# Stick-breaking attention starts without a barrier: the first pair's split parts are made in another buffer

## The chip, the cores and the metric

The kernel runs on one core of one Trainium2 chip. Its time is the device time of one launch in microseconds; the time before is the median of three runs.

## The reference, cut to what matters

The whole program is four transformer layers on 512 tokens of width 1024. The change touches the first layer's mixer, one half of which is stick-breaking attention with 8 heads of 64:

```
xr, gr, q, k, v = split(h @ ev_w_in, 5)            # five panels of 512 columns
q, k = rms_norm(q) * gain, rms_norm(k) * gain      # by head
z   = q @ k.T / 8                                  # for each head
sp  = where(kpos < qpos, softplus(z), 0)
rev = reverse cumulative sum of sp over the keys
w   = exp(where(kpos < qpos, z - rev, -inf))
yb  = w @ v
x  += g1 * (concat([ya, yb]) @ ev_w_out)           # ya: the recurrent half
```

## The kernel before

Every engine walks the same list of steps: gemm stages, norms, attention blocks, and barriers ("bar") at which TensorE (PE), ScalarE (ACT) and VectorE (DVE) wait for one another. Each engine runs its own program in order, and semaphores tie them together. `past(n)` is a semaphore's target of n plus a constant.

**Split operands.** All products are made in float32 from two rounded parts, high = round(x) and low = x - high, as three matmuls. For weights ACT makes the high part (L1604), and GpSimd (POOL) the low part by one subtraction of 128x1024 (L849).

**The panels before the attention.** The normalised q, the normalised k and the values are three "panel" stages, each of four units; a unit is 24 matmuls of 128x512 over four token tiles (L999, L1002, L1005). The k tiles are scaled by DVE (L2380), turned by PE (L972) and taken by ACT (L1642) while PE works on the values' panel. Semaphore `h_take` counts the tiles taken. DVE also finishes the recurrent half during the values' panel: scans (L2434), and the low parts of four output chunks (L2441, `lru_low`). ACT copies the four finished value tiles out of PSUM (L1655, semaphores `evac`).

**The attention, `stick`.** Heads come in four pairs. For a pair, q of both heads is one 128x512 tile, and each head's k is 64 rows of a 128x512 tile whose other 64 rows are zero. All these parts lie in `qk_parts`, which is double buffered by pair and shares its memory with `h_hi` and `h_lo`, the operand of the panels. Before the attention stands a barrier, and behind it three engines work at once: POOL zeroes the other rows (`zero_rows`, two memsets of 64x2048, L875), ACT copies the high parts of pair 0 (`high_parts(0)`, L1821 and L1823) and DVE subtracts for the low parts (`low_parts(0)`, L2450 and L2453). PE then makes the scores of head 0 in four chunks, kt = 2, 1, 0, 3 (L1256 to L1259). ACT takes abs, exp and log of each chunk (L1834, L1837, L1840), DVE adds the softplus (L2466), PE adds the suffix sums (L1270, L1271), ACT makes the weights (L1847), PE multiplies by the values (L1279). Each head's scores are begun before the head in front is done. The output of pair i goes to chunks i + 4 of `y_hi` and `y_lo`, which are empty until then.

**The queue of SyncE (SP).** The output projection is the next gemm stage (its `after_stick` is set). SP issues the loads of its first two weight units, waits for the barrier's three semaphores, and then issues 32 loads of the modulation weights (512 KB each, L544) into a ring of four slots in `tmp`; from the fifth on, each waits for a DVE addition (`ada_add`, L555 and L557), of which DVE makes four for each head.

**POOL's program** is in order too: last panel's weight splits, zeroing, then the low part of the projection's first weight unit (L849).

Of the kernel before, what the change touches and what calls it, by code (L numbers as in the profile page):

```python
# [15 lines left out]
P = 128  # L16
S = 512
# [103 lines left out]
def program(nc, a, out):  # L121
# [13 lines left out]
    with ctx:  # L135
# [98 lines left out]
        def parts(mode):  # L234
# [2 lines left out]
                    [[qkt(4 + 4 * par + k) for k in range(2)] for par in range(2)],  # L237
                    [[qkt(6 + 4 * par + k) for k in range(2)] for par in range(2)])

        def dil_q_high(g, p):  # L240


            if g and p % NB == 0:
                return (yhi, ylo)[g - 1][:, 4 * S:6 * S]
            return whi[1][:, :] if g == 0 else qk[:, (4 * (p % 2) + 2 * (g - 1)) * S:(4 * (p % 2) + 2 * g) * S]
# [159 lines left out]
        panel(ev, 2 * LW, 24, S, a["ev_qn_g"], Q_SCALE)  # L405
        panel(ev, 3 * LW, 28, S, a["ev_kn_g"])
        panel(ev, 4 * LW, 32)
        steps += [("bar", None), ("stick", None), ("mods", 0), ("bar", None)]
        STICK_BAR = sum(kind == "bar" for kind, _ in steps) - 1
        gemm_stage("down", 8, DC, a["ev_w_out"][0], "y", gate=16)  # L410
        steps[-1][1].after_stick = True
        steps[-1][1].products, steps[-1][1].ada = (0, [3]), (0, 8, 8)
# [236 lines left out]
        def stick_z(par, kt):  # L649

            return bank[NB * par + kt][:, 0:S - kt * P]

        def stick_out(par):

            return bank[NB * par + NB - 1][64 * par:64 * par + 64, :]
# [84 lines left out]
        @block.sync  # L740
        def _(sp):
            sp.dma_start(extra[0:DC, 0:P], a["c"].rearrange("b (r n) -> (b r) n", n=P)).then_inc(s_c, 16)
            sp.dma_start(sq9[:, :], a["square"]).then_inc(s_const, 16)

            def first_weights(i):
                if i >= 8:
                    sp.wait_ge(s_first, i - 7)
                sp.dma_start(ring_first[i % 8], ada_source(*first_order[i])).then_inc(s_first_w[i % 8], 16)

            for i in range(4):  # L750
                first_weights(i)
            sp.dma_start(zt(6, 8).rearrange("p (b d) -> p b d", b=NB),
                         a["x"][0].rearrange("(b p) d -> p b d", p=P)).then_inc(s_x, 16)
            for i in range(4, FIRST * DC):
                first_weights(i)
            sp.dma_start(raw[0][:, :].rearrange("p (c n) -> p c n", n=P), stages[0].weights[0](0)).then_inc(w_raw[0], 16)
            sp.dma_start(Z[:, 0:N_MASK * P], a["masks"]).then_inc(s_masks, 16)
            sp.wait_ge(s_zgate, 1)

            for w, name in enumerate(("ev_wa", "ev_wx")):  # L760
                for b in range(2):
                    tiles = Z[64 * b:64 * b + 64, 32 * S:34 * S].rearrange("p (t w n) -> p t w n", w=2, n=P)
                    sp.dma_start(tiles[:, :, w, 64 * b:64 * b + 64],
                                 a[name][0].rearrange("(t b) k j -> b k t j", b=2)[b]).then_inc(s_gates, 16)

            def load(st, i, j):
                u = st.base + j + 2 * i
                half = st.base // 2 + i

                sp.wait_ge(s_wlo, past(u - 1))  # L770
                sp.dma_start(raw[j][:, 0:st.kc * P].rearrange("p (c n) -> p c n", n=S if st.kind == "panel" else P), st.weights[j](i)).then_inc(w_raw[j], 16)

            for st in stages:
                lo = 0
                if st.normed:
                    k = st.gain_index
                    if k >= 2:
                        sp.wait_ge(h_tab, past(k - 1))
                    sp.dma_start(gain_rows[:, DH * (k % 2):DH * (k % 2 + 1)], st.gain.to_broadcast([P, DH])).then_inc(s_gain[k % 2], 16)
                if st.base == 0 or st.after_stick:  # L780
                    if st.base:
                        load(st, 0, 0)
                    load(st, 0, 1)
                    lo = 1
                if st.after_stick:

                    for bar in (bar_pe, bar_act, bar_dve):
                        sp.wait_ge(bar, STICK_BAR)
                    for i in range(4 * DC):
                        ada_load(sp, 0, i)  # L790
                if st.ada[1]:
                    for l in range(st.n):
                        if l >= 2 * lo:
                            load(st, l // 2, l % 2)
                        for i in ada_of(st, l):
                            ada_load(sp, 1, i)
                    continue
                if st.n // 2 - lo <= 1 or st.kind == "panel":
                    for i in range(lo, st.n // 2):
                        load(st, i, 0)  # L800
                        load(st, i, 1)
                else:
                    with sp.Fori(lo, st.n // 2) as i:
                        load(st, i, 0)
                        load(st, i, 1)
            for t in range(NB):
                for hh in range(2):

                    sp.wait_ge(s_xc, DC + 2 * t + hh + 1)
                    sp.dma_start(out[0, t * P:(t + 1) * P, hh * S:(hh + 1) * S], zt(2 * t + hh)).then_inc(s_out, 16)  # L810
            sp.wait_ge(s_out, 16 * 2 * NB)
# [3 lines left out]
        def _(pool):  # L815
# [35 lines left out]
            def zero_rows(n_bars, kind):  # L851
# [5 lines left out]
                    todo = [qk[HALF[1 - par], (4 + 4 * par) * S:(8 + 4 * par) * S].rearrange("p (t n) -> p t n", n=2 * S)[:, :, 0:S] for par in range(2)]  # L857
                elif kind == "diff":
                    todo = [qk[64:128, 5 * S:6 * S], qk[64:128, 7 * S:8 * S], qk[0:64, 9 * S:10 * S], qk[0:64, 11 * S:12 * S]]
                else:  # L860
                    todo = [qk[64:128, 4 * S:8 * S], qk[0:64, 8 * S:12 * S]]
                zero(todo)

            def dil(base):
# [15 lines left out]
            for at_step, (kind, st) in enumerate(steps):  # L880
                if kind == "bar":
                    n_bars += 1
                if kind in ("stick", "diff", "window"):
                    zero_rows(n_bars, kind)
                if kind == "dil":
                    dil(st)
                if kind == "diff":
# [47 lines left out]
        def _(pe):  # L935
# [301 lines left out]

            def stick():
                e = stk
                q_hi, q_lo, k_hi, k_lo = parts("stick")  # L1240
                zero_rows_in(2)

                def scores(i, par, chunks):
                    h = 2 * i + par
                    if par == 0:
                        pe.wait_ge(e["low_parts"], past(2 * i + 2))
                    pe.wait_ge(e["weights"], past(4 * (h - 1)))
                    for kt in chunks:
                        if kt == NB - 1:
                            pe.wait_ge(e["output_low"], past(h - 1))  # L1250
                        if kt == 2 and par and i:
                            products(0, [i - 1])
                        z = stick_z(par, kt)
                        kh, kl = (t[par][i % 2][:, kt * P:(kt + 1) * P] for t in (k_hi, k_lo))
                        qh, ql = (t[i % 2][:, kt * P:S] for t in (q_hi, q_lo))
                        pe.matmul(z, kh, qh, start=True, stop=False)  # L1256
                        pe.matmul(z, kh, ql, start=False, stop=False)
                        pe.matmul(z[:, 0:P], identb[:, :], mask(T_S), start=False, stop=False, skip_group_check=True)
# [264 lines left out]
        def _(act):  # L1523
# [289 lines left out]
            def stick():  # L1813
                e = stk

                q_hi, _, k_hi, _ = parts("stick")

                def high_parts(i):

                    act.wait_ge(e["scores"], past(8 * (i - 1)))  # L1820
                    act.activation(q_hi[i % 2], zt(i + 24), ACT.Copy).then_inc(e["high_parts"], 1)  # L1821
                    for r, t in zip(HALF, k_hi):
                        ins = act.activation(t[i % 2][r, :], zrows(r, i + 28), ACT.Copy)  # L1823
                    ins.then_inc(e["high_parts"], 1)

                def logarithm(i, par, chunks):
# [24 lines left out]
                    act.wait_ge(e["values_added"], past(2 * i + par + 1))  # L1851
                    act.activation(ch(yhi, i + 4)[r, :], stick_out(par), ACT.Copy).then_inc(e["output_high"], 1)

                high_parts(0)
                logarithm(0, 0, STICK_ORDER)
                for h in range(8):
                    i, par = divmod(h, 2)
# [269 lines left out]
        def _(dve):  # L2127
# [254 lines left out]
            def panel(st):  # L2382
# [9 lines left out]
                        head_tile(st, b)  # L2392
                if st.index <= 1:
                    lru_scan(range(2 * st.index, 2 * st.index + 2))
                if st.index in (1, 2):
                    lru_low(range(2 * st.index - 2, 2 * st.index))

# [40 lines left out]
            def lru_low(chunks):  # L2438
                for t in chunks:
                    dve.wait_ge(l_y, t + 1)  # L2440
                    dve.tensor_tensor(ch(ylo, t), zt(16 + t), ch(yhi, t), ALU.subtract)  # L2441

            def stick():
                e = stk

                q_hi, q_lo, k_hi, k_lo = parts("stick")

                def low_parts(i):
                    dve.wait_ge(e["high_parts"], past(2 * i + 1))
                    dve.tensor_tensor(q_lo[i % 2], zt(i + 24), q_hi[i % 2], ALU.subtract).then_inc(e["low_parts"], 1)  # L2450
                    dve.wait_ge(e["high_parts"], past(2 * i + 2))
                    for r, high, low in zip(HALF, k_hi, k_lo):
                        ins = dve.tensor_tensor(low[i % 2][r, :], zrows(r, i + 28), high[i % 2][r, :], ALU.subtract)  # L2453
                    ins.then_inc(e["low_parts"], 1)

                def values(i):
                    dve.wait_ge(e["values_added"], past(2 * i))
# [12 lines left out]
                    dve.wait_ge(e["output_high"], past(2 * i + par + 1))  # L2470
                    dve.tensor_tensor(ch(ylo, i + 4)[r, :], stick_out(par), ch(yhi, i + 4)[r, :], ALU.subtract).then_inc(e["output_low"], 1)

                low_parts(0)
                values(0)
                softplus(0, 0, STICK_ORDER)
                for h in range(8):
# [4 lines left out]
                    if par == 0 and i:  # L2481
                        values(i)
                    if par == 0 and i < 3:
                        low_parts(i + 1)
                    for k in range(4 * par, 4 * par + 3):
                        ada_add(dve, 0, i, k)
                    if h < 7:
# [372 lines left out]
```

## Time and profile before

| what | us |
|---|---|
| median of 3 runs | 2951.89 (2949.53 to 2953.6) |
| time of the profiled execution | 2955.01 |
| its span, first to last instruction | 2953.2 |
| values' panel: last matmul starts | 169.95 |
| attention: first score starts | 174.99 |
| attention: last product of weights and values ends | 260.69 |

All positions are microseconds from the start of the span. The profiled execution is 3.1 us above the median of the runs.

### The profile page before, as it was taken

How to read it: one execution, taken by the hardware profiler on the slowest of the kernel's cores; microseconds unless marked ns; L12 is line 12 of the kernel's file. 1: busy time of each engine (PE TensorE's matmuls, PEld its weight loads, DVE VectorE, ACT ScalarE, POOL GpSimd, SP SyncE). 2: the span in 40 equal slices, each digit the busy share in tenths (PEclk: the TensorE clock that was granted, in tenths of full speed). 3: DMA queues.
4: the chain of work that ended last, by engine and by line, in shares of the span. 5: the costliest groups of instructions: out<-in, count | busy, mean ns of one | idle time of the engine just before them, and what ended most of it. 6: DMA issues, size and time to landing. Idle time of an engine off the chain costs nothing.

```text
span 2953.2 us, 39009 instructions
## 1 busy us (share of the span) xinstructions
PE 2845.3 (96%) x13396; PEld 2322.4 (79%) x13396; DVE 1738.4 (59%) x2097; ACT 1224.3 (41%) x2062; POOL 1076.1 (36%) x486
## 2 busy tenths in 40 slices
PE   6989999999899999999879999999999999999999
PEld 4767788887677888888658888888898889888887
DVE  7476777866566554667465334457666766654333
ACT  3564432223554322244453222256556665532221
POOL 1311344443213444444214444444322442244443
PEclk9999999999999999999899999999999999999999
DMA  6245263643112333333003333332311331133332
GB/s 216 87 157 193 79 197 106 203 126 105 41 29 78 98 94 97 90 94 92 29 8 86 99 93 96 97 95 87 93 30 45 94 89 34 44 97 95 95 97 93
DMA packets 366013, 278.96 MB, mean 94 GB/s; under 512 B 13491, under 2 KB 321076, under 8 KB 365876
## 3 DMA queue, kind: packets, MB, share of 16 engines
q1 hardware_dynamic: 364624, 276.83, 31.2%
q8 instruction: 82, 1.34, 0.2%
q14 instruction: 56, 0.45, 0.1%
q10 hardware_dynamic: 1251, 0.33, 0.0%
HBM read 275.03 MB, written 2.10 MB: 94 GB/s over the span
## 4 chain that ended last, share of the span: by engine, by line
PE 67%; DVE 2%; ACT 2%; issue 1%; POOL 0%; DVEq 0%; ACTq 0%; POOLq 0%
PE banks L1131 13%; PE banks L1126 13%; PE banks L1135 12%; PE banks L999 6%; PE banks L1005 6%; PE banks L1002 6%; PE banks L1395 2%; PE banks L972 1%; PE banks L1456 1%; PE banks L1335 1%; PE banks L1128 1%; PE banks L1324 0%; PE banks L1040 0%; PE banks L1370 0%; PE banks L1369 0%
## 5 line engine op out<-in xcount | busy, mean ns | idle before, releaser
L849 POOL TENSOR_TENSOR w_lo<-w_raw,w_hi 128x1024 fp32r<-128x1024 f32 (+1 forms) x423 | 1027.5, 2429 | 1712.3 <-ACT w_hi L1604 1711.3
L1604 ACT ACTIVATE w_hi<-w_raw 128x1024 fp32r<-128x1024 f32 (+1 forms) x424 | 445.6, 1051 | 1124.9 <-PE banks L1135 804.9
L999 PE MATMUL banks<-w_hi,h_hi 128*128 128x512 f32 x960 | 386.4, 403 | 1.4 <-ACT h_hi L1782 1.4
L1005 PE MATMUL banks<-w_lo,h_hi 128*128 128x512 f32 x960 | 376.9, 393 | 0.7 <-POOL w_lo L849 0.7
L1002 PE MATMUL banks<-w_hi,h_lo 128*128 128x512 f32 x960 | 375.9, 392 | 0.7 <-DVE h_lo L587 0.7
L1126 PE MATMUL banks<-h_hi,w_hi 128*128 128x512 f32 x1280 | 340.1, 394 | 6.9 <-ACT h_hi L1782 6.9
L1131 PE MATMUL banks<-h_lo,w_hi 128*128 128x512 f32 x1280 | 321.3, 391 | 2.6 <-DVE h_lo L587 2.4
L1126 PEld LDWEIGHTS banks<-h_hi,w_hi 128*128 128x128 f32 x1280 | 241.7, 189 | 65.2 <-issue 8.7
L1131 PEld LDWEIGHTS banks<-h_lo,w_hi 128*128 128x128 f32 x1280 | 240.3, 188 | 57.9 <-DVE h_lo L587 8.6
L1135 PE MATMUL banks<-h_hi,w_lo 128*128 128x512 f32 x1152 | 284.5, 389 | 0.0
L1135 PEld LDWEIGHTS banks<-h_hi,w_lo 128*128 128x128 f32 x1152 | 216.2, 188 | 44.9
L1126 PE MATMUL banks<-mid_hi,w_hi 128*128 128x512 f32 x864 | 220.3, 394 | 7.2 <-ACT mid_hi L1734 4.7
L1005 PEld LDWEIGHTS banks<-w_lo,h_hi 128*128 128x128 f32 x960 | 196.2, 204 | 35.5 <-POOL w_lo L849 1.5
L999 PEld LDWEIGHTS banks<-w_hi,h_hi 128*128 128x128 f32 x960 | 196.5, 205 | 32.6 <-issue 2.1
L1002 PEld LDWEIGHTS banks<-w_hi,h_lo 128*128 128x128 f32 x960 | 196.9, 205 | 31.8 <-DVE h_lo L587 1.0
L1131 PE MATMUL banks<-mid_lo,w_hi 128*128 128x512 f32 x864 | 218.3, 391 | 2.3 <-DVE mid_lo L2275 2.1
L2292 DVE TENSOR_TENSOR xT<-banks,xT 128x512 f32 (+1 forms) x80 | 55.3, 692 | 273.2 <-PE banks L1135 273.1
L1135 PE MATMUL banks<-mid_hi,w_lo 128*128 128x512 f32 x864 | 214.4, 389 | 0.0
L1126 PEld LDWEIGHTS banks<-mid_hi,w_hi 128*128 128x128 f32 x864 | 160.6, 188 | 45.3 <-ACT mid_hi L1734 8.1
L1131 PEld LDWEIGHTS banks<-mid_lo,w_hi 128*128 128x128 f32 x864 | 162.2, 188 | 41.4 <-DVE mid_lo L2275 4.7
L1135 PEld LDWEIGHTS banks<-mid_hi,w_lo 128*128 128x128 f32 x864 | 162.2, 188 | 33.5
L2380 DVE TENSOR_TENSOR tmp<-tmp,head_sums 128x512 f32<-128x512 f32 (+1 forms) x84 | 133.5, 1589 | 34.2 <-issue 23.2
(343 smaller groups left out, 4256.2 us busy)
## 6 DMA issues: line engine op xcount, KB each, us to landing
Z<-in_ada_w SPq DMA_DIRECT2D x64, 512.0 KB, 5.0
w_raw<-in_m_w_up SPq DMA_DIRECT2D x64, 512.0 KB, 4.0
w_raw<-in_m_w_down SPq DMA_DIRECT2D x64, 512.0 KB, 3.8
w_raw<-in_kv_w SPq DMA_DIRECT2D x48, 512.0 KB, 3.7
w_raw<-in_ffn_w_gate SPq DMA_DIRECT2D x44, 512.0 KB, 3.7
w_raw<-in_ffn_w_up SPq DMA_DIRECT2D x44, 512.0 KB, 3.7
tmp<-in_ada_w SPq DMA_DIRECT2D x32, 512.0 KB, 4.5
w_raw<-in_ffn_w_down SPq DMA_DIRECT2D x32, 512.0 KB, 3.8
```

The lines of the kernel that those rows point to most:

```text
L849: pool.tensor_tensor(wlo[j][:, 0:n], raw[j][:, 0:n], whi[j][:, 0:n], ALU.subtract).then_inc(s_wlo, 1)
L972: mm = pe.transpose(turned(n)[:, j * P:(j + 1) * P], tmp[4 + n % 2][:, j * P:(j + 1) * P], ident)
L999: pe.matmul(t, hh, wh, start=k == 0, stop=False)
L1002: pe.matmul(t, hl, wh, start=False, stop=False)
L1005: mm = pe.matmul(t, hh, wl, start=False, stop=k == DC - 1)
L1126: pe.matmul(g, whi[par][:, k * P:(k + 1) * P], hi[:, k * S:(k + 1) * S], start=(k == 0), stop=False)
L1131: mm = pe.matmul(g, whi[par][:, k * P:(k + 1) * P], lo[:, k * S:(k + 1) * S], start=False, stop=early and k == st.kc - 1)
L1135: mm = pe.matmul(g, wlo[par][:, k * P:(k + 1) * P], hi[:, k * S:(k + 1) * S], start=False, stop=(k == st.kc - 1))
L1395: mm = pe.matmul(o, dil_vals[:, at:at + P], dil_probs[q % 2][:, own:own + width], start=g == 0 and c == 0, stop=g == 2 and c == NB - 1, sk ...
L1604: act.activation(whi[par][:, 0:kc * P], raw[par][:, 0:kc * P], ACT.Copy).then_inc(s_whi, 1)
L2292: dve.tensor_tensor(x, G[par], x, ALU.add).then_inc(evac[par], 1)
L2380: dve.tensor_tensor(by_head(tmp[4 + n % 2], w), roped, scale, ALU.mult).then_inc(h_out, 1)
```

## The change

The first barrier goes. Pair 0's parts are made in chunks 5, 6 and 7 of `y_hi` and `y_lo`, all of them on DVE within its part of the values' panel. POOL zeroes the rows of `qk_parts` once the panel's last matmul is done; PE waits for that only at head 2, the first head that reads `qk_parts`. PE waits for the copies of the value tiles before its second chunk. SP issues the modulation weights' loads once all q and k tiles are taken.

```diff
+        def first_parts():
+            return ch(yhi, 5), ch(ylo, 5), [ch(yhi, 6), ch(yhi, 7)], [ch(ylo, 6), ch(ylo, 7)]
...
-        steps += [("bar", None), ("stick", None), ("mods", 0), ("bar", None)]
-        STICK_BAR = sum(kind == "bar" for kind, _ in steps) - 1
+        steps += [("stick", None), ("mods", 0), ("bar", None)]
+        stick_values = panels[-1]
...
+        def stick_parts(i):
+            if i == 0:
+                return first_parts()
+            q_hi, q_lo, k_hi, k_lo = parts("stick")
+            return q_hi[i % 2], q_lo[i % 2], [t[i % 2] for t in k_hi], [t[i % 2] for t in k_lo]
...
                 if st.after_stick:
-                    for bar in (bar_pe, bar_act, bar_dve):
-                        sp.wait_ge(bar, STICK_BAR)
+                    sp.wait_ge(h_take, past(stick_values.tiles))
...
-                if kind in ("stick", "diff", "window"):
+                if kind in ("diff", "window"):
                     zero_rows(n_bars, kind)
+                if kind == "stick":
+                    pool.wait_ge(gemm, past(stick_values.base + stick_values.n))
+                    zero([qk[64:128, 4 * S:8 * S], qk[0:64, 8 * S:12 * S]])
...
             def stick():                                   # PE
-                zero_rows_in(2)
+                pe.wait_ge(h_take, past(stick_values.tiles))
                 def scores(i, par, chunks):
                     h = 2 * i + par
+                    q_hi, q_lo, k_hi, k_lo = stick_parts(i)
+                    if h == 2 and chunks[0] == STICK_ORDER[0]:
+                        zero_rows_in(2)
...
+                        if h == 0 and kt == 1:
+                            for b in range(NB):
+                                pe.wait_ge(evac[b % 2], past(tile_evac(stick_values, b) + 1))
...
-                high_parts(0)                              # ACT
                 logarithm(0, 0, STICK_ORDER)
...
                 if st.index <= 1:                          # DVE, panel
                     lru_scan(range(2 * st.index, 2 * st.index + 2))
+                if st is stick_values:
+                    stick_first()
                 if st.index in (1, 2):
                     lru_low(range(2 * st.index - 2, 2 * st.index))
...
             def lru_low(chunks):
                 for t in chunks:
                     dve.wait_ge(l_y, t + 1)
-                    dve.tensor_tensor(ch(ylo, t), zt(16 + t), ch(yhi, t), ALU.subtract)
+                    ins = dve.tensor_tensor(ch(ylo, t), zt(16 + t), ch(yhi, t), ALU.subtract)
+                link(ins)
+
+            def stick_low(i):
+                e = stk
+                q_hi, q_lo, k_hi, k_lo = stick_parts(i)
+                dve.wait_ge(e["high_parts"], past(2 * i + 1))
+                dve.tensor_tensor(q_lo, zt(i + 24), q_hi, ALU.subtract).then_inc(e["low_parts"], 1)
+                dve.wait_ge(e["high_parts"], past(2 * i + 2))
+                for r, high, low in zip(HALF, k_hi, k_lo):
+                    ins = dve.tensor_tensor(low[r, :], zrows(r, i + 28), high[r, :], ALU.subtract)
+                ins.then_inc(e["low_parts"], 1)
+
+            def stick_first():
+                q_hi, _, k_hi, k_lo = stick_parts(0)
+                for c in range(2):
+                    for t in (k_hi[c], k_lo[c]):
+                        dve.memset(t[HALF[1 - c], :].bitcast(F32), 0.0)
+                dve.wait_ge(h_take, past(stick_values.tiles))
+                dve.wait_ge(h_out, past(stick_values.tiles))
+                dve.tensor_copy(q_hi, zt(24)).then_inc(stk["high_parts"], 1)
+                for r, t in zip(HALF, k_hi):
+                    ins = dve.tensor_copy(t[r, :], zrows(r, 28))
+                ins.then_inc(stk["high_parts"], 1)
+                stick_low(0)
...
-                low_parts(0)                               # DVE, stick
+                for b in range(NB):
+                    dve.wait_ge(evac[b % 2], past(tile_evac(stick_values, b) + 1))
                 values(0)
                 softplus(0, 0, STICK_ORDER)
```

`link` makes DVE wait until its own instruction has written.

## Rows read from the trace of the kernel before

**Rows 1.** The page, busy time of PE: us, share of the span, instructions.
```profile
PE 2845.3 (96%) x13396; PEld 2322.4 (79%) x13396; DVE 1738.4 (59%) x2097; ACT 1224.3 (41%) x2062; POOL 1076.1 (36%) x486
```

**Rows 2.** Timeline, PE, 152 to 186: start, us, what, [idle before, releaser].
```profile
169.95 0.39 PE L1005 MATMUL banks<-w_lo,h_hi 128*128 128x512 f32 x1
174.99 0.55 PE L1256 MATMUL banks<-qk_parts 128*128 128x256 f32 x1 [4.64 <-POOL qk_parts L875]
...
178.87 0.34 PE L1256 MATMUL banks<-qk_parts 128*128 128x256 f32 x1
...
182.09 0.49 PE L1271 MATMUL banks<-Z,squares 128*128 128x128 f32 x2 [1.04 <-DVE Z L2466]
```

**Rows 3.** Timeline, POOL and SP, 152 to 186.
```profile
171.12 3.66 POOL L875 MEMSET qk_parts<- 64x2048 f32 x2 [9.00 <-ACTq L1548]
175.01 2.36 POOL L849 TENSOR_TENSOR w_lo<-w_raw,w_hi 128x1024 fp32r<-128x1024 f32 x1 [0.23 <-POOL qk_parts L875]
...
171.08 14.87 SPq L544 DMA_DIRECT2D tmp<-in_ada_w  x5
```

**Rows 4.** Timeline, ACT, 152 to 186.
```profile
165.47 0.58 ACT L1642 ACTIVATE Z<-banks 128x512 f32<-128x512 f32 x1
...
170.38 0.60 ACT L1655 ACTIVATE Z<-banks 128x512 f32<-128x512 f32 x1 [0.40 <-PE banks L1005]
171.17 0.63 ACT L1821 ACTIVATE qk_parts<-Z 128x512 fp32r<-128x512 f32 x1 [0.20 <-issue]
171.71 1.25 ACT L1823 ACTIVATE qk_parts<-Z 64x512 fp32r<-64x512 f32 x2
176.24 0.39 ACT L1834 ACTIVATE Z<-banks 128x256 f32<-128x256 f32 x1 [3.29 <-PE banks L1259]
```

**Rows 5.** Timeline, DVE, 152 to 186.
```profile
167.77 2.49 DVE L2441 TENSOR_TENSOR y_lo<-Z,y_hi 128x512 fp32r<-128x512 f32 x4
171.93 0.69 DVE L2450 TENSOR_TENSOR qk_parts<-Z,qk_parts 128x512 fp32r<-128x512 f32 x1 [1.68 <-ACT qk_parts L1821]
172.99 1.39 DVE L2453 TENSOR_TENSOR qk_parts<-Z,qk_parts 64x512 fp32r<-64x512 f32 x2 [0.36 <-ACT qk_parts L1823]
174.41 0.65 DVE L2458 TENSOR_SCALAR Z<-Z 128x512 f32<-128x512 f32 x1
177.56 0.42 DVE L2466 SCALAR_TENSOR_TENSOR Z<-banks,Z 128x256 f32<-128x256 f32 x1 [2.50 <-ACT Z L1840]
```

**Rows 6.** Timeline, DVE and POOL, 2117 to 2128, a later stage with the same forms.
```profile
2118.14 0.42 DVE L2645 CAST y_hi<-Z 64x512 fp32r<-64x512 f32 x1
2118.61 0.48 DVE L2644 MEMSET y_lo<- 64x512 f32 x1
2119.11 1.99 DVE L2645 CAST y_lo<-Z 64x512 fp32r<-64x512 f32 x1
...
2118.36 2.46 POOL L849 TENSOR_TENSOR w_lo<-w_raw,w_hi 128x1024 fp32r<-128x1024 f32 x1 [4.00 <-ACT w_hi L1604]
```

**Rows 7.** The same stretch, where POOL comes up between two DVE subtractions.
```profile
2123.13 0.68 DVE L2563 TENSOR_TENSOR Z_rounded<-Z,y_hi 128x512 fp32r<-128x512 f32 x1
2123.73 2.89 DVE L2563 TENSOR_TENSOR Z_rounded<-Z,y_lo 128x512 fp32r<-128x512 f32 x1
...
2123.51 2.55 POOL L849 TENSOR_TENSOR w_lo<-w_raw,w_hi 128x1024 fp32r<-128x1024 f32 x1 [2.69 <-ACT w_hi L1604]
```

**Rows 8.** Timeline, DVE and POOL, 2167 to 2169.
```profile
2167.60 0.82 DVE L2690 CAST w_hi<-Z 64x512 fp32r<-64x512 f32 x1 [2.69 <-PE banks L1005]
...
2167.63 0.52 POOL L875 MEMSET w_hi<- 64x512 f32 x1 [11.14 <-PE banks L1005]
2168.21 0.69 POOL L875 MEMSET w_lo<- 64x512 f32 x1
```

**Rows 9.** Windows just after PE restarts: stretch, us, busy by engine, PEclk (granted share), DMA.
```profile
174.90:178.20 3.30, 3.21 (x12) 2.32 (x12) 0.58 (x2) 1.86 (x5) 2.36 (x1) 0.50 0.94 364
...
1434.30:1441.10 6.80, 6.80 (x28) 5.48 (x28) 3.48 (x6) 1.83 (x8) 0.20 (x1) 0.50 0.00 0
```

More of the change, by code:

```diff
@@ L859, in zero_rows @@
                     todo = [qk[64:128, 5 * S:6 * S], qk[64:128, 7 * S:8 * S], qk[0:64, 9 * S:10 * S], qk[0:64, 11 * S:12 * S]]
-                else:
-                    todo = [qk[64:128, 4 * S:8 * S], qk[0:64, 8 * S:12 * S]]
                 zero(todo)
@@ L1239, in stick @@
                 e = stk
-                q_hi, q_lo, k_hi, k_lo = parts("stick")
-                zero_rows_in(2)
+                pe.wait_ge(h_take, past(stick_values.tiles))
                 def scores(i, par, chunks):
                     h = 2 * i + par
+                    q_hi, q_lo, k_hi, k_lo = stick_parts(i)
+                    if h == 2 and chunks[0] == STICK_ORDER[0]:
+                        zero_rows_in(2)
                     if par == 0:
@@ L1252, in scores @@
                             products(0, [i - 1])
+                        if h == 0 and kt == 1:
+                            for b in range(NB):
+                                pe.wait_ge(evac[b % 2], past(tile_evac(stick_values, b) + 1))
                         z = stick_z(par, kt)
-                        kh, kl = (t[par][i % 2][:, kt * P:(kt + 1) * P] for t in (k_hi, k_lo))
-                        qh, ql = (t[i % 2][:, kt * P:S] for t in (q_hi, q_lo))
+                        kh, kl = (t[par][:, kt * P:(kt + 1) * P] for t in (k_hi, k_lo))
+                        qh, ql = (t[:, kt * P:S] for t in (q_hi, q_lo))
                         pe.matmul(z, kh, qh, start=True, stop=False)
@@ L1814, in stick @@
                 e = stk
-                q_hi, _, k_hi, _ = parts("stick")
                 def high_parts(i):
+                    q_hi, _, k_hi, _ = stick_parts(i)
                     act.wait_ge(e["scores"], past(8 * (i - 1)))
-                    act.activation(q_hi[i % 2], zt(i + 24), ACT.Copy).then_inc(e["high_parts"], 1)
+                    act.activation(q_hi, zt(i + 24), ACT.Copy).then_inc(e["high_parts"], 1)
                     for r, t in zip(HALF, k_hi):
-                        ins = act.activation(t[i % 2][r, :], zrows(r, i + 28), ACT.Copy)
+                        ins = act.activation(t[r, :], zrows(r, i + 28), ACT.Copy)
                     ins.then_inc(e["high_parts"], 1)
@@ L2440, in lru_low @@
                     dve.wait_ge(l_y, t + 1)
-                    dve.tensor_tensor(ch(ylo, t), zt(16 + t), ch(yhi, t), ALU.subtract)
+                    ins = dve.tensor_tensor(ch(ylo, t), zt(16 + t), ch(yhi, t), ALU.subtract)
[21 more added lines that the diff above has]
+                stick_low(0)
             def stick():
                 e = stk
[L2446 to L2454, printed above, removed]
                 def values(i):
@@ L2483, in stick @@
                     if par == 0 and i < 3:
-                        low_parts(i + 1)
+                        stick_low(i + 1)
                     for k in range(4 * par, 4 * par + 3):
```

## The prediction

> **What bounds the kernel now.** I read the page's busy times first: PE is busy for 96% of the span [rows 1], so a change pays where it takes time out of PE's row and not elsewhere. Then the timeline of PE around the barrier that goes. The values' panel ends at 169.95 + 0.39 = 170.34, the first score starts at 174.99, and the row gives 4.64 us of idle time, released by POOL's memset [rows 2]. That hole is all that the change can remove. Its neighbours show what fills it. ACT copies the last value tile at 170.38, then makes the high parts until 171.71 + 1.25 = 172.96 [rows 4]. DVE makes the low parts until 172.99 + 1.39 = 174.38 [rows 5]. POOL zeroes from 171.12 to 171.12 + 3.66 = 174.78 [rows 3]. Three waits end there, POOL's last, DVE's only 0.4 us ahead of it. The first thing to see: taking POOL off this path alone is worth 0.4 us, because DVE is next in line.
>
> Behind the first score (call its start T) comes a chain that a later start shifts as a whole: first softplus on DVE at T + 2.57 (177.56) [rows 5], first suffix sum at T + 7.10 (182.09), where PE has waited 1.04 us for DVE [rows 2].
>
> **Part by part: when can DVE deliver?** The high parts move from ACT to DVE, so T now hangs on DVE alone. ACT is rid of 0.63 + 1.25 us of copies [rows 4], which is worth nothing by itself: it then sat idle 3.29 us before its first abs [rows 4].
>
> *What stands in front on DVE.* The k tiles are all taken at 165.47 + 0.58 = 166.05 [rows 4], well within the panel. But DVE is busy with the recurrent half: its four L2441 subtractions begin at 167.77, one each 0.61 (from 2.49 for four, the last taking 0.69) [rows 5]. Two of them stay in front of the new work and end at 167.77 + 0.61 + 0.69 = 169.07; the other two move behind it. The new `link` adds a wait of DVE for its own write. I estimate it at 0.2 us, as POOL's end to PE's start (174.78 to 174.99) [rows 2, 3], bounds 0 and 0.3. So the new work starts at 169.3.
>
> *Four memsets of 64x512.* One takes 0.48 and its follower starts 0.50 later [rows 6]; with an overlap as L2441 has, 0.41. I take 0.45: 1.8 us, until 171.1. The last two meet POOL. The row at 2118.61 is such a memset beside POOL's subtraction and took its 0.48 [rows 6]; beside a POOL memset no row shows one. I take no delay; were the third held as a copy is, all behind it would queue once more, 1.3 us for bound (its own end at 172.5, and three copies behind L849).
>
> *Three copies.* A CAST of 64x512 takes 0.42 [rows 6], and the 128x512 one has as many elements in a partition, so undisturbed they are 3 x 0.42 = 1.3 us. They are not undisturbed. POOL no longer waits for a barrier but for the panel's last matmul, 170.34, and starts at about 170.42, as ACT's value copy, released by the same matmul, did at 170.38 [rows 4] (bounds 170.4 and 170.6). Its two memsets are 1.8 us each [rows 3], so POOL writes from 170.4 to 174.1 at least, just where DVE copies. The trace shows what a copy does then. The cast at 2119.11 comes while POOL's subtraction (2118.36 to 2120.82) runs, takes 1.99 in place of 0.42 and ends 0.28 after POOL [rows 6]. The cast at 2167.60 stands beside a POOL memset, ends at 2168.42, 0.27 after that memset's end at 2168.15; and the next memset, which takes 0.52 alone, takes 0.69, until the cast is through [rows 8]. L2458, a one-input operation too, started at 174.41 and ended at 175.06, 0.28 after the memset's end at 174.78 [rows 3, 5]. So a DVE copy and a POOL memset shut each other out.
>
> The Trainium skill ("SBUF — State Buffer", "Who interferes with whom") says the same of copies, and that a DVE instruction with two SBUF inputs contends only with GpSimd instructions that read. The Trainium skill ("GPSIMD Engine Reference", "Key points") also names contention with two SBUF inputs, but without that limit; by it the subtractions at 171.93 and 172.99 would have been held until the memsets' ends at 172.92 and 174.78, and the rivals below that let subtractions meet a memset would be dearer by up to 1.8 us, the sum not. They took 0.69 each beside the memsets [rows 3, 5], so the trace bears out the first.
>
> *Who goes first when both wait?* That settles the sum. At 2123.13 a DVE subtraction runs, POOL's comes up at 2123.51, DVE's next one at 2123.73, directly behind. POOL's ended at 2126.06 and takes 2.36 alone [rows 3], so it ran from 2123.7; DVE's ended at 2126.62, 0.56 after it [rows 7]. The one that waited first was served first, and a gapless chain of DVE did not keep POOL out. I take this for copies against memsets too:
> - q copy: issued 171.1, held by memset 1 (170.42 to 172.22), ends 172.50.
> - memset 2 comes up 0.06 behind the first [rows 8], waits from 172.28 and runs 172.50 to 174.30. The first k copy ends 0.28 later, 174.58.
> - POOL starts its L849 0.23 behind the memset [rows 3], 174.53, in front of the second k copy, and takes 2.36: 176.9. The copy ends at 177.2. Were the copy first, L849 would hold the two-input subtractions instead, as at 2123.73, with the same end within 0.2.
> - Three subtractions, 0.61 + 0.69 + 0.69 [rows 5] = 2.0: 179.2, and 0.2 to PE: T = 179.4.
>
> So T goes from 174.99 to 179.4: the barrier's hole of 4.6 us becomes a hole of 9.1 us that ends on DVE, and the sum is **+4.4 us**.
>
> *The rest at nothing, and what covers it.* The two L2441 behind the new work, their link and L2458 are at most 0.61 + 0.69 + 0.2 + 0.65 = 2.2 us after the low parts [rows 5]; the first softplus comes 2.57 + 0.2 us after them, so 0.6 us of cover; without it the softplus would be late by what is over. L849, which the zeroing now precedes by a different wait, is wanted only at the projection, more than 80 us on. SP's ring loads start near 166.1 in place of 171.08, but only four fit, and the fifth waits for a DVE addition: five issues took 14.87 us [rows 3]. No gain, and the additions keep their place behind the softplus. PE's new wait for the value tiles before the second chunk ends at 170.98 [rows 4], long past. At head 2, two heads of 85.7 / 8 = 10.7 us on (85.7 is worked out below), POOL has long zeroed.
>
> *The clock.* After the hole PE ran at half clock (0.50, that is 1.2 of 2.4 GHz) in 174.9 to 178.2 [rows 9], and its first four groups of scores took 3.88 us [rows 2]. It will fall again. Elsewhere a restart stayed at 0.50 for 6.8 us [rows 9]. PE must do seven groups by T + 7.1; at 0.50 they take about 3.9 + 3.5 = 7.4. I add 0 to 0.5 and leave 0 in the sum.
>
> Everything else shifts as a whole. The profile's own 2955.01 (span 2953.2) becomes 2959.4; the median of the runs, 3.1 us lower, becomes 2951.89 + 4.4 = 2956.3. A tenth of a per cent is 3.0 us, and what a measurement can tell here from no change is about 0.2%, 5.9 us.
>
> **Rivals.**
> 1. *DVE keeps its turn.* The three copies go through in a row once memset 1 is done: 172.50, 172.92, 173.35; memset 2 does not hold the subtractions, which end at 175.4; T = 175.6, +0.6 us, 2952.5. For it: nobody has seen copies in a row against a memset; against it, [rows 7].
> 2. *Faster: no meeting.* If the copies go undisturbed (DVE is early by 0.6 and ahead of POOL, or the memset lets them by), they end at 172.4, the subtractions at 174.4, T = 174.6, a gain of 0.4 us, 2951.5. It decides from an end of the subtractions before 174.78. Even at best DVE begins at 169.07, so a gain past 1 us is excluded, and one past 0.2% (the whole hole and the slow clock behind it) too. Against it: [rows 6, 8].
> 3. *Slower by more than 0.2%: the clock.* A hole twice as long leaves PE at 0.50 into the suffix sums. Each slow us there costs half a us, as the work of two takes one at full clock. It decides at 1.5 us beyond the sum, thus with the 0.3 us of the scores and 2.4 us of slow sums, a slow stretch to about T + 9.5; 6.8 us is the longest that the rows show. It would give 2958 to 2960.
>
> **How the numbers follow.** Forecast (+4.4) 0.66, rival 1 0.12, rival 2 0.11, rival 3 0.11. The forecast's own range is +3.0 to +5.7 (start of POOL, memsets, clock, each taken at a share of its bound), 2954.9 to 2957.6, and a median of few runs can miss by 1 us. To leave out 2 in 10 the range must take in rival 1 and most of rival 2: 2951.0 to 2958.3. Of the forecast's weight some 0.03 lies past 5.9 us. Slower by over 0.2%: 0.14; faster: 0.01; within: 0.85.
>
> **What the changed profile would show.** Right: the idle time before the first L1256 is 9 us and ends on a DVE subtraction, not on POOL; the new DVE casts show 1.3 to 2.6 us where 0.42 would do; a POOL memset starts near 170.4, L849 near 174.5; SP's first ring load stands near 166. The distance from the first score to the end of the last product of weights and values (260.69, the table of times) stays 260.69 - 174.99 = 85.7 us. Wrong: casts at 0.42 and a hole of 4 us (rival 2), one long cast and then two short (rival 1), or PE at 0.50 past T + 7 (rival 3). Wrong altogether would be a DVE that reaches the memsets well before 169, or a later stage that gives or takes the shift.

## The result, and the profile after

The changed kernel takes 2958.62 us (median of 20 runs, 2955.11 to 2961.02), the kernel before 2953.85 (20 runs, 2949.53 to 2958.98). The ratio is 1.0014, 95% interval 1.0008 to 1.0020: slower by 4.8 us by the medians. The forecast was +4.4 us. Its absolute time, 2956.3, lies 2.3 us low, nearly all of it because the kernel before, measured more often, came out 2.0 us above the median that the forecast started from. For the same reason the time lies 0.3 us past the top of the stated range, 2951.0 to 2958.3. Counted from the kernel before as measured here, it is inside: +4.8 us, where the range goes to +6.4.

A line of code has another number in each version: L1256 of the kernel before is L1270 here and L1271 in e1. PE's timeline around the start of the attention (start, us, what, [idle before, releaser]), to be held against [rows 2]:

```profile
169.51 0.39 PE L1014 MATMUL banks<-w_lo,h_hi 128*128 128x512 f32 x1
178.98 0.55 PE L1270 MATMUL banks<-y_hi 128*128 128x256 f32 x1 [9.08 <-issue]
...
186.11 0.49 PE L1285 MATMUL banks<-Z,squares 128*128 128x128 f32 x2 [0.36 <-DVE Z L2495]
```

The hole of 4.64 us has become one of 9.08 us, and the barrier is not in it. The row names no releaser ("issue"), so it does not say whom PE waits for; DVE's timeline does, for its last subtraction ends at 177.50 + 1.38 = 178.88, 0.10 before PE starts (in e6 below the same wait does name DVE):

```profile
167.32 1.29 DVE L2455 TENSOR_TENSOR y_lo<-Z,y_hi 128x512 fp32r<-128x512 f32 x2
168.77 0.48 DVE L2473 MEMSET y_hi<- 64x512 f32 x1 [0.17 <-DVE y_lo L2455]
...
170.48 0.48 DVE L2473 MEMSET y_lo<- 64x512 f32 x1
170.89 1.37 DVE L2476 CAST y_hi<-Z 128x512 fp32r<-128x512 f32 x1
172.19 4.67 DVE L2478 CAST y_hi<-Z 64x512 fp32r<-64x512 f32 x2
176.90 0.69 DVE L2462 TENSOR_TENSOR y_lo<-Z,y_hi 128x512 fp32r<-128x512 f32 x1
177.50 1.38 DVE L2465 TENSOR_TENSOR y_lo<-Z,y_hi 64x512 fp32r<-64x512 f32 x2
```

Three copies that take 0.42 us each elsewhere [rows 6] take 1.37 + 4.67 = 6.0 us here. POOL's rows in the same stretch, and the first of the two k copies by itself, asked for in a narrower stretch:

```profile
169.97 2.02 POOL L881 MEMSET qk_parts<- 64x2048 f32 x1 [8.29 <-PE banks L1014]
172.04 1.97 POOL L881 MEMSET qk_parts<- 64x2048 f32 x1
174.24 2.34 POOL L857 TENSOR_TENSOR w_lo<-w_raw,w_hi 128x1024 fp32r<-128x1024 f32 x1 [0.23 <-POOL qk_parts L881]
...
172.19 2.10 DVE L2478 CAST y_hi<-Z 64x512 fp32r<-64x512 f32 x1
```

The ends come in pairs: POOL's three instructions end at 171.99, 174.01 and 176.58; DVE's three copies end at 172.26, 174.29 and 176.86, each 0.27 or 0.28 us behind one of them. The rest is as it was, but for SP: its first ring load comes at 165.64, 4.3 us ahead of the panel's end, where it came 0.7 behind it. The first softplus and suffix sum keep their distance from the first score (186.11 - 178.98 = 7.13, before 7.10).

### The profile page after: what moved, and what is told of

Read it like the earlier page. It is cut to its first block, busy times and chain, and to the rows that moved or that the text cites. A ratio compares the mean times of both kernels' runs of the same rounds, so it can differ in the third digit from the quotient of the medians.

```text
span 2955.3 us, 39011 instructions
## 1 busy us (share of the span) xinstructions
PE 2843.7 (96%) x13396; PEld 2322.4 (79%) x13396; DVE 1738.1 (59%) x2104; ACT 1222.7 (41%) x2059; POOL 1077.3 (36%) x486
## 4 chain that ended last, share of the span: by engine, by line
PE 67%; DVE 2%; ACT 2%; issue 1%; POOL 0%; DVEq 0%; ACTq 0%; POOLq 0%
PE banks L1140 13%; PE banks L1135 13%; PE banks L1144 12%; PE banks L1008 6%; PE banks L1014 6%; PE banks L1011 6%; PE banks L1409 2%; PE banks L981 1%; PE banks L1470 1%; PE banks L1349 1%; PE banks L1137 1%; PE banks L1338 0%; PE banks L1049 0%; PE banks L1384 0%; PE banks L1383 0%
## 5 line engine op out<-in xcount | busy, mean ns | idle before, releaser
L2297 DVE TENSOR_TENSOR mid_lo<-tmp,mid_hi 128x512 f32 (+1 forms) x64 | 122.2, 1909 | 56.1 <-ACT mid_hi L1748 56.1
```

The lines of the kernel that those rows point to most:

```text
L2297: dve.tensor_tensor(ch(mlo, l), tmp[1], ch(mhi, l), ALU.subtract).then_inc(r_lo, 1)
```

## The experiments

Since the panel ends at slightly different places from run to run (168.5 to 171.1 on the traces' clocks), I compare two lengths: PE's idle time before the first score, and the way from the end of the panel's last matmul to the first suffix sum. Before: 4.64 and 11.75 us. Changed: 9.08 and 16.21, so the start of the attention costs 4.5 us more. e2, e3, e4 and e8 were run once each and are read from their traces alone; the others have ratios from 11 or 12 runs.

**e1, POOL behind the low parts.** The changed kernel, with one wait more on POOL.

```diff
                     pool.wait_ge(gemm, past(stick_values.base + stick_values.n))
+                    pool.wait_ge(stk["low_parts"], past(2))
                     zero([qk[64:128, 4 * S:8 * S], qk[0:64, 8 * S:12 * S]])
```

> The changed kernel, but POOL begins its two memsets (and so its L849 split behind them) only once DVE has made all of pair 0's parts. Nothing is left out. Theory (POOL's three instructions hold DVE's copies): the three copies take 0.42 us each, PE's idle time before the first score falls from 9.08 us to about 4.4, and the time falls by some 4.7 us against the changed kernel, to 0 to 1 us below the kernel before. Rival (DVE is late by its own work, with or without POOL): the idle time stays near 9 us.

The DVE timeline of e1, and its first score:

```profile
172.05 0.35 DVE L2477 CAST y_hi<-Z 128x512 fp32r<-128x512 f32 x1
172.33 0.84 DVE L2479 CAST y_hi<-Z 64x512 fp32r<-64x512 f32 x2
173.20 0.69 DVE L2463 TENSOR_TENSOR y_lo<-Z,y_hi 128x512 fp32r<-128x512 f32 x1
173.81 1.38 DVE L2466 TENSOR_TENSOR y_lo<-Z,y_hi 64x512 fp32r<-64x512 f32 x2
...
175.29 0.36 PE L1271 MATMUL banks<-y_hi 128*128 128x256 f32 x1 [4.24 <-issue]
```

Idle time 4.24, way 10.90. The way is 5.3 us shorter than in the changed kernel. The ratio to the kernel before is 1.0000 (0.9991 to 1.0009). The same work in the same place on DVE, and the loss is gone; the rival, that DVE is late by its own work, falls. Its own work does account for what is left: the idle time is no better than the barrier's by more than 0.4 us.

**e2, only the split behind the low parts.** The wait of e1, placed behind the two memsets.

> The changed kernel, but only POOL's third instruction, the split of 128x1024, waits for pair 0's low parts; the two memsets stay where they are. Theory: the q copy waits for memset 1, the first k copy for memset 2, the second k copy for nothing; idle time before the first score about 7.0 us (9.08 less the 2.3 us of the split, and 0.2 for the meeting). Rival (the memsets do not let a copy in between and a copy waits once for the whole train, or the split never mattered): it stays at 9 us or falls under 5.

```profile
171.96 2.53 DVE L2479 CAST y_hi<-Z 64x512 fp32r<-64x512 f32 x2
176.61 0.55 PE L1271 MATMUL banks<-y_hi 128*128 128x256 f32 x1 [6.95 <-issue]
```

Idle time 6.95, way 14.08: POOL's split was worth 2.1 us of the hole, the two memsets 6.95 - 4.24 = 2.7.

**e3, eight small memsets.**

```diff
-                    zero([qk[64:128, 4 * S:8 * S], qk[0:64, 8 * S:12 * S]])
+                    zero([qk[r, k * S:(k + 1) * S] for r, first in ((slice(64, 128), 4), (slice(0, 64), 8)) for k in range(first, first + 4)])
...
-                        zero_rows_in(2)
+                        zero_rows_in(8)
```

> The changed kernel, but POOL zeroes the same rows with eight memsets of 64x512 in place of two of 64x2048. Theory (each of DVE's copies waits for the one POOL instruction that is ahead of it, and no more): every copy waits at most 0.5 us, they end near 173 on the trace's clock and the idle time is 5.0 to 5.5 us. Rival 1 (DVE keeps its turn once it has it): the copies after the first take 0.42 each, idle time 4.6 to 4.8. Rival 2 (POOL's train as a whole goes first): 9 us or more.

```profile
169.15 5.28 POOL L881 MEMSET qk_parts<- 64x512 f32 x8 [8.28 <-PE banks L1014]
170.08 0.67 DVE L2476 CAST y_hi<-Z 128x512 fp32r<-128x512 f32 x1
170.68 1.56 DVE L2478 CAST y_hi<-Z 64x512 fp32r<-64x512 f32 x2
...
174.36 0.55 PE L1270 MATMUL banks<-y_hi 128*128 128x256 f32 x1 [5.27 <-issue]
```

Idle time 5.27. The k copies take 0.78 each, neither 0.42 (DVE keeps its turn) nor the whole of POOL's 5.28 us (POOL keeps its). They take turns, and a turn is one instruction, so its length is what a copy pays. In the changed kernel and in e3 the one whose turn it was had also come up first each time, so the runs do not tell strict turns from first come, first served. Rival 1 of the prediction, with the k copies at 0.42, falls.

**e4, the high parts on ACT.** The three copies leave DVE; POOL stays as in the changed kernel.

```diff
+                    if st is stick_values and l == 1:          # ACT, panel
+                        act.activation(first_parts()[0], zt(24), ACT.Copy).then_inc(stk["high_parts"], 1)
+                    if st is stick_values and l == 3:
+                        act.wait_ge(h_take, past(st.tiles))
+                        for r, t in zip(HALF, first_parts()[2]):
+                            ins = act.activation(t[r, :], zrows(r, 28), ACT.Copy)
+                        ins.then_inc(stk["high_parts"], 1)
...
-                dve.tensor_copy(q_hi, zt(24)).then_inc(stk["high_parts"], 1)
...
```

> The changed kernel, with one thing moved: the three high parts of pair 0 are made by ACT within the values' panel, so that DVE has four memsets and three subtractions left and no copy. POOL is as in the changed kernel. Theory (copies and POOL's memsets shut each other out, DVE memsets and two-input subtractions beside POOL memsets do not): all seven DVE instructions take their undisturbed time though POOL zeroes beside them, and the idle time before the first score is about 3.3 us. Rival (POOL holds any DVE instruction that touches two SBUF operands): the subtractions wait for the memsets, idle time 6 us or more.

```profile
169.21 3.66 POOL L881 MEMSET qk_parts<- 64x2048 f32 x2 [8.27 <-PE banks L1014]
170.15 0.62 DVE L2469 TENSOR_TENSOR y_lo<-Z,y_hi 128x512 fp32r<-128x512 f32 x1
170.70 1.37 DVE L2472 TENSOR_TENSOR y_lo<-Z,y_hi 64x512 fp32r<-64x512 f32 x2
...
172.17 0.35 PE L1270 MATMUL banks<-y_hi 128*128 128x256 f32 x1 [3.03 <-issue]
```

Idle time 3.03, way 9.60. The subtractions run at full pace in the middle of POOL's memsets.

**e8, copies with two inputs.** The same three results by max(x, x), still on DVE, POOL still beside it.

```diff
-                dve.tensor_copy(q_hi, zt(24)).then_inc(stk["high_parts"], 1)
+                dve.tensor_tensor(q_hi, zt(24), zt(24), ALU.max).then_inc(stk["high_parts"], 1)
                 for r, t in zip(HALF, k_hi):
-                    ins = dve.tensor_copy(t[r, :], zrows(r, 28))
+                    ins = dve.tensor_tensor(t[r, :], zrows(r, 28), zrows(r, 28), ALU.max)
```

> The changed kernel, but DVE makes the three high parts by max(x, x) of two SBUF inputs in place of a copy; the result is the same. POOL is as in the changed kernel. Theory (a two-input instruction passes beside POOL's memset and is held only by POOL's split, which reads): the three take 0.69 us each beside the memsets, POOL's memsets take 1.80 and not 2.0, the split comes at about 4 us behind the panel's end and holds the one subtraction that is left, idle time before the first score about 7 us; were that one through before the split, 5 us. Rival (what holds DVE is any POOL instruction): about 9 us as in the changed kernel or more.

```profile
170.24 3.65 POOL L881 MEMSET qk_parts<- 64x2048 f32 x2 [8.27 <-PE banks L1014]
171.18 0.62 DVE L2476 TENSOR_TENSOR y_hi<-Z 128x512 fp32r<-128x512 f32 x1
171.73 1.37 DVE L2478 TENSOR_TENSOR y_hi<-Z 64x512 fp32r<-64x512 f32 x2
...
173.74 3.43 DVE L2465 TENSOR_TENSOR y_lo<-Z,y_hi 64x512 fp32r<-64x512 f32 x2
174.13 2.49 POOL L857 TENSOR_TENSOR w_lo<-w_raw,w_hi 128x1024 fp32r<-128x1024 f32 x1 [0.23 <-POOL qk_parts L881]
177.27 0.55 PE L1270 MATMUL banks<-y_hi 128*128 128x256 f32 x1 [7.09 <-issue]
```

Idle time 7.09. An instruction that is slower alone (0.69 for 0.42) makes the hole 2 us shorter. Both POOL memsets are back to 1.8 us each, and the two L2465 take 3.43 in place of 1.38: the split, which reads SBUF, holds the second one, where the memsets, which only write, held none.

**e6, the clock kept up.** The changed kernel with 34 bf16 matmuls in the hole, `keep_rate(34)`, behind PE's first wait; their results are not used.

> The changed kernel, with 34 matmuls of 128x512 (bf16, results unused) put on PE into the hole before the first score. Theory: the granted clock stays at 1.00, the first score starts at the same time as in the changed kernel within 0.2 us, and the time from it to the first suffix sum falls from 7.1 us to about 6.5, since only the first group of four matmuls lies on the path (1.22 against 0.7 us); the whole gets 0.5 to 2 us faster. Rival (the slow clock carries much of the loss): more than 3 us faster.

The first score of e6, whose wait names its releaser:

```profile
178.44 0.38 PE L1271 MATMUL banks<-y_hi 128*128 128x256 f32 x1 [1.71 <-DVE y_lo L2466]
```

Windows of e6 (stretch, us, busy of PE, PEld, DVE, ACT, POOL, granted share, DMA): the added matmuls, the rest of the hole, and the scores.

```profile
169.30:176.70 7.40, 7.40 (x35) 3.14 (x34) 7.17 (x6) 0.60 (x1) 6.35 (x3) 1.00 0.37 146
176.80:178.40 1.60, 0.00 (x0) 0.00 (x0) 1.57 (x3) 0.00 (x0) 0.00 (x0) 1.00 0.00 0
178.50:179.50 1.00, 1.00 (x8) 0.79 (x8) 1.00 (x2) 0.28 (x1) 0.00 (x0) 1.00 0.00 0
179.60:182.90 3.30, 3.30 (x14) 2.59 (x13) 1.52 (x4) 3.14 (x8) 0.00 (x0) 0.50 0.00 0
```

First score to first suffix sum is 185.03 - 178.44 = 6.6 us, as expected, but the clock did not stay up: it fell 1.1 us after the scores had begun. The ratio to the kernel before is 1.0013 (1.0002 to 1.0023), the changed kernel's is 1.0014. So no gain that can be told. Since 3.4 us at half clock were left, e6 alone does not settle the rival, that the slow clock carries much of the loss. The distances from the first score to the first suffix sum do, up to that point. Where the first chunk ran at half clock it is 7.10 us (before) and 7.13 (changed); where it ran at full clock it is 6.66 (e1) and 6.59 (e6). The slow clock costs some 0.5 us there, and the kernel before pays it too, so it is no part of the difference.

**e7, the loads alone.** The kernel before, with its barrier; only SP waits for `h_take` in place of the barrier.

> The kernel before, with its barrier, and of the change only SP's part: the modulation weights' loads are issued once the q and k tiles are taken, not at the barrier. Theory: the first load is issued 5 us earlier, the first softplus and the first DVE addition stand where they stood, the time is that of the kernel before within 0.1%. Rival (the loads gate DVE's additions): 1 us or more faster.

The ratio is 0.9995 (0.9985 to 1.0005), the idle time 4.64 us, released by POOL's memset as before. The first ring load is issued at 164.21, 4.2 us before the panel's end (168.46), where before it came 0.7 us behind it; nothing follows from it.

**e5 and e9, the parts made early.** What the runs point to. On top of e4, POOL zeroes the empty rows of the output chunks right behind its last split of the panel, and DVE subtracts ahead of the recurrent half's low parts instead of behind them.

```diff
+                    pool.wait_ge(s_wlo, past(stick_values.base + stick_values.n))
+                    zero([t[HALF[1 - c], :] for c in range(2) for t in (first_parts()[2][c], first_parts()[3][c])])
                     pool.wait_ge(gemm, past(stick_values.base + stick_values.n))
...
-                if st is stick_values:                     # DVE, panel
+                if st.next is stick_values:
                     stick_first()
...
                 pe.wait_ge(h_take, past(stick_values.tiles))
+                zero_rows_in(4)
```

> A version meant to beat both: the barrier stays away as in the changed kernel, but ACT makes the high parts while the values' panel runs (q in its second unit, k behind the last take), POOL zeroes the empty rows of the output chunks right after its last split of the panel, and DVE subtracts the low parts directly behind its last scan, ahead of the recurrent half's low parts; no DVE copy or memset is left there. Theory: the low parts are ready at about the panel's last matmul, PE is idle 0.2 to 0.5 us before the first score and stays at full clock, and the time is 4.5 to 6.5 us below the kernel before, 9 to 11 below the changed one. Rival (what goes in front delays ACT's value copies or DVE's softplus, so the wait comes back one step later): the idle time before the first score falls, but the distance from the first score to the first suffix sum grows beyond 7.1 us by as much.

> The same kernel as in e5 (parts made early by ACT, POOL and DVE), timed again for a narrower interval. Theory: the ratio to the kernel before is again 0.998 to 0.999, since the way from the panel's last matmul to the first suffix sum is 5.4 us shorter in the traces; a ratio of 1.000 or more would say that a later stage gives the gain back.

The timeline of e5: the panel's last matmul, the first score, its second chunk, the first suffix sum; then DVE's subtractions and its copy of the values, and POOL.

```profile
168.25 0.40 PE L1016 MATMUL banks<-w_lo,h_hi 128*128 128x512 f32 x1
168.49 0.28 PE L1273 MATMUL banks<-y_hi 128*128 128x256 f32 x1
...
169.43 0.41 PE L1273 MATMUL banks<-y_hi 128*128 128x384 f32 x1 [0.30 <-ACT Z L1672]
...
174.99 0.49 PE L1288 MATMUL banks<-Z,squares 128*128 128x128 f32 x2 [1.50 <-DVE Z L2498]
...
166.67 1.38 DVE L2475 TENSOR_TENSOR y_lo<-Z,y_hi 64x512 fp32r<-64x512 f32 x2
...
168.78 3.67 POOL L881 MEMSET qk_parts<- 64x2048 f32 x2 [6.04 <-PE banks L1016]
170.73 1.99 DVE L2490 TENSOR_SCALAR Z<-Z 128x512 f32<-128x512 f32 x1
```

The low parts end at 168.05, before the panel does, and the scores follow without a gap. The way from the panel's end to the first suffix sum is 6.34 us, 5.4 less than before. The one-input copy of the values is still held by a memset (1.99 us for 0.43), but the chain of logarithms on ACT covers it: first score to first suffix sum is 6.50 us. The ratio to the kernel before is 0.9990 (0.9981 to 0.9999) in the first set and 0.9991 (0.9982 to 1.0000) in the second, some 2.8 us by the mean of the two ratios (the medians differ by 4.8 and by 1.7). It is the fastest of the versions timed more than once. The gain is smaller than the 5.4 us of the traces and than the 4.5 to 6.5 us expected, and both intervals all but reach the kernel before. Where the other 2.6 us are is not shown: the intervals reach to 0.9981 and 0.9982, which would be 5.6 and 5.3 us, so the whole gain may be there, and that a part of it is given back later stays open.

## Why the prediction was right

Its steps, as distances from the end of the panel's last matmul:

| step | forecast | measured |
|---|---|---|
| POOL's first memset starts | 0.1 | 0.07 |
| q copy issued | 0.8 | 0.99 |
| q copy ends | 2.2 | 2.36 |
| first k copy ends | 4.2 | 4.39 |
| second k copy ends | 6.9 | 6.96 |
| subtractions end | 8.9 | 8.98 |
| first score | 9.1 | 9.08 |

- *DVE is next in line behind POOL, and has older work in front.* Right. The link cost 0.17 for an estimated 0.2; the memsets 2.1 us from the first start to the q copy for 1.8, as gaps of 0.06 to 0.15 stand between them. It did not matter, since the q copy had to wait for memset 1 anyway. DVE's memsets themselves were not held by POOL. POOL's first memset took 2.02 us, 0.2 more than any term had; the steps from the q copy's end to PE took 6.72 for 6.90, so the 9.08 agrees with the 9.1 better than its terms do.
- *A copy and a POOL memset shut each other out.* Shown by e1 (nothing on POOL, 4.24), e4 (no copies, 3.03) and e8 (two-input copies pass).
- *The one that waited first is served first, one instruction a turn.* One instruction a turn is shown by the pairs of ends in the changed trace and by e3; the order of service fits this rule and strict turns alike. Rival 1 (0.12) is excluded: the first k copy, issued directly behind the q copy, still let memset 2 go first. So is rival 2: no copy went undisturbed.
- *The split counts too.* 2.1 us in e2, forecast 2.3 with the meeting.
- *The loads at nothing.* e7.
- *The clock at nothing.* It was slow until 183.8, 4.8 us after PE started again (3.5 us before), inside the 6.8 us of [rows 9]. The longer stretch used up idle time: PE waited 0.36 us before the first suffix sum, where it had waited 1.04, and the sum came 7.13 us after the first score. Rival 3, with its 0.11, asked for a slow stretch to T + 9.5 and did not come about.
- *Everything behind shifts as a whole.* Borne out by the medians (+4.8 us, interval 2.4 to 5.9), not by the two profiled executions: there the span grew by 2.1 us only. From the first suffix sum to the projection's first matmul the kernel before takes 80.5 us, the changed one 78.9, with the same 372 matmuls:

```profile
182.00:262.50 80.50, 76.10 (x372) 51.39 (x372) 62.76 (x83) 57.54 (x133) 0.00 (x0) 0.98 0.64 201
202.50:205.50 3.00, 3.00 (x10) 2.08 (x11) 2.84 (x4) 2.52 (x6) 0.00 (x0) 0.50 0.17 48
```

```profile
186.00:265.00 79.00, 74.52 (x372) 50.26 (x372) 62.78 (x83) 57.51 (x133) 0.00 (x0) 1.00 0.65 205
206.50:209.50 3.00, 3.00 (x20) 2.42 (x19) 2.84 (x4) 2.75 (x7) 0.00 (x0) 1.00 0.17 48
```

(The first fence is the kernel before, the second the changed one; the second line of each is the same part of the attention, 27.5 us behind the first score.) The kernel before ran 3.4 us at half clock there, from 202.2 to 205.6, and the changed one did not. So the 85.7 us that the forecast said would stay became 84.15, by a term that the sum did not have. Whether this is chance or belongs to the kernel is open. The stretch stands at this place in the traces of the kernel before, e1, e5, e7 and e9, and in none of the changed kernel, e2, e3, e4, e6 and e8. e5 and e9, one kernel twice, agree on it and differ elsewhere: e9 has two more such stretches, near 219 and near 260, and e5 has none there. The rest, some 0.8 us of the 4.5, lies outside the attention and was not looked for. The verdict rests on the medians of 20 runs each, not on the two spans.

## What to carry to other kernels

When a barrier goes, list what each engine will do in its place and lay the instructions of DVE and POOL side by side: a barrier also keeps them apart. Here 4.6 us of waiting turned into 9.1 because three one-input DVE copies alternated with three long POOL instructions; moving the copies to ACT and the subtractions ahead of less urgent work on the same queue did what removing the barrier was to do. And before work is put on an engine, look at what already stands in its queue at that moment: with POOL out of the way DVE still delivered only 0.4 us sooner than the barrier did.

## What the runs showed of the hardware that was not expected

- A POOL memset that meets DVE copies takes longer too. The second memset of the changed kernel took 1.97 us (1.80 each beside two-input instructions in e4 and e8): it came up at 172.04, while the q copy was not through. In e3 the three memsets that came up while a copy was not through took 0.69, all later ones 0.52. The first one's 2.02 us has another cause, which is open, for in e3 the first took 0.75 and ended at 169.90, before the first copy started at 170.08:

```profile
169.15 0.75 POOL L881 MEMSET qk_parts<- 64x512 f32 x1 [8.28 <-PE banks L1014]
```

- 7.4 us of back-to-back matmuls did not protect the clock in e6: after them PE was idle for 1.7 us, worked for 1.1 us at full clock, and then ran at 0.50 for 3.3 us. In e5, where PE had no gap but the 0.30 and 1.50 us shown, the scores stood at 0.28 us for 256 columns from the first on, and the granted clock was 1.00 until 196. An idle time of 3.03 us in e4 was followed by no slow stretch either, and one of 4.24 us in e1 by one that began 0.5 us after PE had started again.
- Single stretches of some 3.4 us at half clock stand in the midst of the attention, where PE is busy without a gap (202.50 to 205.50 above). Their number differs from trace to trace, for one kernel too: one between 190 and 262 in e5, three in e9, so that the mean granted clock there was 0.98 and 0.93. Each costs up to 1.7 us, so two spans that differ by 2 us say little about an edit.
